# Row sums of the masked attention split between TensorE and GpSimd in the second stack

## The reference

```python
s = einsum(q, k) * scale + rel_bias            # keys by queries
p = exp(s - rowmax)                            # masked keys are 0
o = (p @ v) / sum(p over keys)                 # the row sum is the subject here
```

## Time and profile before

| | |
|---|---|
| three runs, median (lowest to highest) | 2995.5 us (2989.74 to 2997.5) |
| span of the profiled execution | 2989.5 us |
| the run nearest to it | 2989.74 us, 0.24 above the span |
| PE busy | 2868.7 us, 96% |
| DVE, ACT, POOL busy | 1429.5, 1061.5, 245.2 us |
| mean granted clock of PE | 0.973 |
| loops of the stage, first layer and second | from about 1682 to 1825, and from about 2429 to 2572 |

### The profile page before, as it was taken

The page is one execution under the profiler, slowest core; times in us unless marked ns, Lnnn a source line. Parts: engine busy times, 40 slices in busy tenths (PEclk is TensorE's granted clock), DMA queues, the critical chain, the costliest instruction groups (busy, mean ns, idle before and its releaser), DMA issues. The chain is left out here.

```text
span 2989.5 us, 46483 instructions
## 1 busy us (share of the span) xinstructions
PE 2868.7 (96%) x18586; PEld 2453.5 (82%) x18586; DVE 1429.5 (48%) x2279; ACT 1061.5 (36%) x1478; POOL 245.2 (8%) x222
## 2 busy tenths in 40 slices
PE   8999999999999999999999889999999988999998
PEld 7986899999897789999877546788887754678886
DVE  3743477742673267782333654433433355443342
ACT  3244433322334443332333333422323333343232
POOL 1001300001100220001100022000010002200001
PEclk9998999999998999999999889999999988999999
DMA  3200322222220132223232001222222200122222
GB/s 123 99 29 16 133 85 86 92 88 86 76 85 15 43 124 95 84 75 107 88 132 96 29 1 55 86 91 94 98 104 95 96 29 1 57 85 98 92 92 111
DMA packets 44784, 237.04 MB, mean 79 GB/s; under 512 B 4894, under 2 KB 14750, under 8 KB 21872
## 3 DMA queue, kind: packets, MB, share of 16 engines
q1 hardware_dynamic: 34976, 222.09, 21.1%
q10 hardware_dynamic: 9680, 13.17, 1.3%
HBM read 233.09 MB, written 11.59 MB: 82 GB/s over the span
## 5 line engine op out<-in xcount | busy, mean ns | idle before, releaser
L161 PE MATMUL psum<-u_up_a_hi,w_a_hi 128*128 128x264 f32 x1408 | 376.3, 287 | 6.1 <-DVE u_up_a_lo L1900 5.0
L162 PE MATMUL psum<-u_up_a_lo,w_a_hi 128*128 128x264 f32 x1408 | 373.1, 285 | 0.0
L152 DVE TENSOR_TENSOR w_mlp_b_lo<-ring,w_mlp_b_hi 128x1024 fp32r<-128x1024 f32 x128 | 156.9, 1226 | 329.9 <-ACT w_mlp_b_hi L145 329.9
L152 DVE TENSOR_TENSOR w_a_lo<-ring,w_a_hi 128x1024 fp32r<-128x1024 f32 (+1 forms) x154 | 187.6, 1219 | 208.8 <-ACT w_a_hi L145 206.3
L164 PE MATMUL psum<-u_up_a_hi,w_a_lo 128*128 128x264 f32 x1408 | 286.2, 284 | 0.0
L161 PEld LDWEIGHTS psum<-u_up_a_hi,w_a_hi 128*128 128x128 f32 x1408 | 265.1, 188 | 14.2 <-DVE u_up_a_lo L1900 9.7
L145 ACT ACTIVATE w_a_hi<-ring 128x1024 fp32r<-128x1024 f32 (+1 forms) x154 | 161.4, 1049 | 293.4 <-PE psum L164 292.1
L162 PEld LDWEIGHTS psum<-u_up_a_lo,w_a_hi 128*128 128x128 f32 x1408 | 264.7, 188 | 0.1
L145 ACT ACTIVATE w_mlp_b_hi<-ring 128x1024 fp32r<-128x1024 f32 x128 | 135.6, 1060 | 300.4 <-PE psum L164 299.7
L164 PEld LDWEIGHTS psum<-u_up_a_hi,w_a_lo 128*128 128x128 f32 x1408 | 219.4, 189 | 0.0
L161 PE MATMUL psum<-u_up_b_hi,w_mlp_b_hi 128*128 128x512 f32 x512 | 199.6, 390 | 1.0 <-DVE u_up_b_lo L502 1.0
(11 more groups left out here) (459 smaller groups left out, 6505.3 us busy)
## 6 DMA issues: line engine op xcount, KB each, us to landing
ring<-in_wup SPq DMA_DIRECT2D x44, 1024.0 KB, 4.9
ring<-in_wup_b SPq DMA_DIRECT2D x32, 1024.0 KB, 4.8
ring<-in_wdown_b SPq DMA_DIRECT2D x32, 1024.0 KB, 4.8
ring<-in_win SPq DMA_DIRECT2D x22, 1024.0 KB, 4.9
ring<-in_wdown SPq DMA_DIRECT2D x32, 704.0 KB, 4.1
ring<-in_win_b SPq DMA_DIRECT2D x12, 1024.0 KB, 4.8
near_copies<-near_rows ACTq DMA_DIRECT2D x2, 4608.0 KB
ring<-in_wout SPq DMA_DIRECT2D x8, 1024.0 KB, 4.9
```

What stands on the lines that cost most here:

```text
L152: nc.vector.tensor_tensor(W["lo"][:, buf, 0:n], W["tiles"][:, slot, at:at + n], W["hi"][:, buf, 0:n].bitcast(F32), ALU.subtract).then_inc( ...
L161: nc.tensor.matmul(out[c], a_hi, b_hi, start=start, stop=False)
L162: nc.tensor.matmul(out[c], a_hi, b_lo, start=False, stop=False)
```

## The change

A new buffer `acc` holds 256 columns for each of the two heads, which stand for queries 256 to 511. POOL copies step 0's probabilities into its second half and step 1's first 128 columns into its first half. It adds step 1's other 128 columns, and then adds step 2's columns 128 to 383 (`last_sum`). PE no longer reads `prob` for the row sums in steps 0 and 1. In step 2 it reads only the 128 columns that `acc` doesn't cover, in step 3 all 512, and then `acc` (256). That is 896 columns a head and unit.

PE waits in mix(n,3) for POOL's last sum. ACT waits, before it overwrites a buffer of `prob`, until POOL has read it. On POOL `first_sums(n+1)` stands ahead of the multiplication for unit n, and `last_sum(n+1)` right behind that multiplication.

```diff
             def mix(n, step):
+                if step == K - 1:
+                    pe.wait_ge(summed.sem, summed.at(layer, SUMS + 4 * n + 4))
                 pass_waits(pe, S)
-                for bank, at in ((6, (u["v"], u["v"] + 2 * DH)), (7, (u["v"] + DH, u["v"] + DH))):
+                ones = v[:, j, u["v"] + DH:u["v"] + 2 * DH]
+                for h in range(2):
+                    at = u["v"] + 2 * DH * h
+                    mm = nc.tensor.matmul(ps[DH * h:DH * (h + 1), 6, c0:TB], v[:, j, at:at + DH], prob[:, g % 2, h, 0:TB - c0],
+                                          start=(step == 0), stop=(step == K - 1), skip_group_check=True)
+                if step >= 2:
+                    end = TB if step == K - 1 else 2 * P
                     for h in range(2):
-                        mm = nc.tensor.matmul(ps[DH * h:DH * (h + 1), bank, c0:TB], v[:, j, at[h]:at[h] + DH],
-                                              prob[:, g % 2, h, 0:TB - c0],
-                                              start=(step == 0), stop=(step == K - 1), skip_group_check=True)
+                        mm = nc.tensor.matmul(ps[DH * h:DH * (h + 1), 7, c0:end], ones, prob[:, g % 2, h, 0:end - c0],
+                                              start=(step == 2), stop=False, skip_group_check=True)
+                if step == K - 1:
+                    for h in range(2):
+                        mm = nc.tensor.matmul(ps[DH * h:DH * (h + 1), 7, 2 * P:TB], ones, acc[:, h, :],
+                                              start=False, stop=True, skip_group_check=True)
...
             def exponent(n, step):
+                if step == 0 and n:
+                    act.wait_ge(summed.sem, summed.at(layer, SUMS + 4 * n))
+                if step == 2:
+                    act.wait_ge(summed.sem, summed.at(layer, SUMS + 4 * n + 1))
+                if step == 3:
+                    act.wait_ge(summed.sem, summed.at(layer, SUMS + 4 * n + 3))
...
+            def first_sums(n):
+                g = K * n
+                pool.wait_ge(probs.sem, probs.at(layer, g + 1))
+                if n:
+                    pool.wait_ge(mixed.sem, mixed.at(layer, g))
+                nc.gpsimd.tensor_copy(acc[:, :, P:2 * P], prob[:, g % 2, :, 0:P]).then_inc(summed.sem, 1)
+                pool.wait_ge(probs.sem, probs.at(layer, g + 2))
+                nc.gpsimd.tensor_copy(acc[:, :, 0:P], prob[:, (g + 1) % 2, :, 0:P]).then_inc(summed.sem, 1)
+                pool.wait_ge(summed.sem, summed.at(layer, SUMS + g + 1))
+                nc.gpsimd.tensor_tensor(acc[:, :, P:2 * P], acc[:, :, P:2 * P], prob[:, (g + 1) % 2, :, P:2 * P],
+                                        ALU.add).then_inc(summed.sem, 1)
+
+            def last_sum(n):
+                g = K * n
+                pool.wait_ge(probs.sem, probs.at(layer, g + 3))
+                pool.wait_ge(summed.sem, summed.at(layer, SUMS + g + 3))
+                nc.gpsimd.tensor_tensor(acc[:, :, :], acc[:, :, :], prob[:, g % 2, :, P:3 * P], ALU.add).then_inc(summed.sem, 1)
+
+            first_sums(0)
+            last_sum(0)
             for n, u in enumerate(UNITS_B[:-1]):
                 out = part_y[:, :] if u.get("onto") else y[:, u["y"], :]
+                first_sums(n + 1)
                 pool.wait_ge(copied.sem, copied.at(layer, n + 1))
                 pool.wait_ge(inverted.sem, inverted.at(layer, n + 1))
                 then(nc.gpsimd.tensor_tensor(out, out, sums[:, :], ALU.mult))
                 at += 1
+                last_sum(n + 1)
                 if "gate" in u:
...
```

More of the change, by code:

```diff
@@ L2659, in attend_stage_b @@
     side_pe, side_act, side_dve, cleared = S["side_pe"], S["side_act"], S["side_dve"], S["pool_side"]
+    acc, summed, SUMS = M["acc"], S["pool_side"], 6 + 2
     gate_pe, gate_out = S["gate_pe"], S["gate_out"]
@@ L3278, in second_stack @@
             side_pe=signal("side_pe", 8), side_act=signal("side_act", 9), side_dve=signal("side_dve", 21),
-            gate_pe=signal("gate_pe", 6), gate_out=signal("gate_out", 6), pool_side=signal("pool_side", 6 + 2))
+            gate_pe=signal("gate_pe", 6), gate_out=signal("gate_out", 6), pool_side=signal("pool_side", 6 + 2 + 4 * len(UNITS_B)))
         U = len(UNITS_B)
@@ L3317, in mixer @@
                     own = Scope(nc, attention)
-                    for name, shape in (("prob", [P, 2, 2, TB]), ("cn", [P, TB]), ("pc", [P, TB])):
+                    for name, shape in (("prob", [P, 2, 2, TB]), ("cn", [P, TB]), ("pc", [P, TB]), ("acc", [P, 2, TB // 2])):
                         M[name] = own.sb("at_" + name, shape)
```

## The result

The change made the kernel slower: 3028.6 us in the median of 6 runs (3016.1 to 3039.3), against 2996.5 for the kernel before (6 runs, 2989.7 to 2998.6). The ratio on record is 1.0096, 95% interval 1.0075 to 1.0118; the quotient of these two medians, 1.0107, lies inside it. The forecast was 2995, its range 2984 to 3010.

What follows compares the result with a forecast made beforehand. DVE was taken to set the pace from mix(n,0) to mix(n,1), PE's columns from there to mix(n,3). Loop terms summed to -0.2 us a layer, -0.4 for two, from median 2995.5 to 2995; range 2984 to 3010.

Steps and rivals of the forecast that it cites:

- The prediction's own sign of being wrong: Clock falls in the two stages not eight, or POOL's copies and additions taking much more than 0.5, 0.73, 1.28 us.
- Rival 1: Loop 6: PE idles about 3 us ahead of mix(6,3), one more clock fall a layer; 3004.5 us, chance 0.24.
- Rival 2: Loop 5: the thin stretch gets fuller, one clock fall less in each layer; 2985.5 us, chance 0.17.
- Rival 4: PE's columns bound everywhere and POOL hides all; 2983 us, with L3018 down to 2974; chance 0.07.
- Rival 3: DVE's cast is held by POOL's instruction; 3.8 us more, 2999 us, chance 0.17.
- PE's columns at full clock: Steps 1 and 2 each save 0.43 us, step 3 costs 0.43; step 0's 0.21 is worth nothing.
- L3018: DVE's join falls from 0.79 to 0.16 us, 0.63 earlier up to mix(n,1), in loops 1 to 6 and 8.
- The cast: DVE's cast with one SBUF input is taken as not held by POOL; if held, loop 4 is 0.6 us slower.
- POOL's own times: Copies of 256 columns 0.5 us (bounds 0.31 and 0.73), additions 0.73 and 1.28; 3.0 us a unit.
- Loop 3: POOL's gate and addition of unit 2 delay DVE's two-input chain with `select`, and loop 4's bias behind it; +1.0 us.
- The square: `norm_square` waits for POOL's addition onto `y`, now behind the last sum; loop 6 +2.2 us, loop 8 +0.4.
- The end: POOL does gate, addition and low part behind unit 9's last sum, with nothing covering this; +1.8 us.

Runs made afterwards that it cites:

- e5: The kernel before without PE's row sums of steps 0 and 1 (384 of 1280 columns a unit), nothing in their place; ratio 1.0012.
- e14: e5 with constant matmuls of the same length in the places of the columns left out; ratio 1.0015.
- e2: The kernel before with only PE's columns of the change, `acc` holding ones, no POOL work or wait for it; 3020.1 us, ratio 1.0096.
- e13: e9 with PE's columns as in e2; 3004.7 us, ratio 1.0034.
- e9: The kernel before with POOL's multiplication waiting until DVE's join L3018 is over; 2981.2 us, ratio 0.9951.
- e1: The changed kernel's POOL sums and all its waits, but PE's columns as in the kernel before; 3015.9 us, ratio 1.0066.
- e10: e7 with POOL's multiplication also waiting until DVE's splits of the next unit are done, where no square waits for it; ratio 1.0129.
- e6: The kernel before with 256 columns of zeros added to step 3, nothing taken away; ratio 1.0027.
- e7: The changed kernel with POOL's addition onto `y` ahead of the next unit's last sum for units 5 and 7; 3020.6 us, ratio 1.0075.
- e12: e9 with six (loop 7) and four (loop 8) constant matmuls ahead of score(n+1,1), where PE waits for DVE's maxima; 2968.9 us, ratio 0.9902.
- e15: e2 with constant matmuls of the same length in the places of the missing columns in steps 0 to 2; 3035.9 us, ratio 1.0131.
- e3: The changed kernel with three constant matmuls of 128 columns ahead of transposed(n,2); ratio 1.0172.
- e16: The kernel before with only step 2's 256 columns of row sums moved into step 3; 3007.5 us, ratio 1.0031.

## Why the prediction was wrong

**The step that failed** is the sum's silence on the clock: "There are four falls in the loops of a layer", and the sum went by the waits and columns with the falls as they were. In the first layer four became six and in the second four became five, and they grew from 58 to 126 us in all. The prediction's own sign of being wrong came: the falls in the two stages were eleven and not eight. A fall of 10.2 us cost 4.7, 0.46 per us at half clock; 75 us more of it make some 34 us, by the 0.40 of the 88 executions 30, against 27.6 measured in the stages. So the clock is large enough to carry the loss. That taking columns off PE brings the falls about is shown by taking away (e5) and filling again (e14), and by moving (e2, e13 against e9). POOL's waits lose time too (e1, 1.0066), and how the loss of the whole divides between the two halves is open, since they overlap.

**The rivals.** Rival 1 had the right effect, more falls, with the wrong cause, place and size. It put one fall in loop 6, after an idle time of PE of 3 us ahead of mix(6,3), which the wait for POOL was to bring. That idle time was 0.52 us. The falls begin in loop 4, where no idle time of PE ahead of the fall is above 0.90 us, and e2 has them with no wait on POOL at all. Its rule from the Trainium skill (TensorE: Matmul & The Clock Gate, Why this matters for your kernels) warned in the right direction, but speaks of idle gaps; here it was fewer columns in a stream that was already thin. Rival 2 (a fall less in loop 5) did not come in this kernel. Its reasoning was sound for the join alone: e9, with the 0.63 us and all the columns, has no fall in loop 5. Rival 4 (columns are worth 12.8 us) is refuted by e2 and e5. Rival 3 holds: the cast is held. The Trainium skill's GPSIMD Engine Reference (Specifications) names such contention for a 2-port mode; no run shows whether the cast runs in one. The rival's price of 3.8 us was not measured by itself, since e10, which freed the cast, moved other waits.

**PE's columns at full clock.** Forecast -0.43 in loop 2, measured 0.0. The pieces were right (mix of step 0 0.44, step 3 +0.43 by e6, and steps 0 and 1 together -0.44 by e5, which is step 1's part). The error was to count step 2's 0.43 as a gain, though the turning of the maxima right behind it waits for DVE's splits.

**L3018.** Forecast 0.79 to 0.16 and 0.63 a loop; measured 0.164 in the mean, and 0.62 to 0.63 in loop 2 (e1, e9 and after alike). Right, and the best part of the change.

**The cast.** Forecast "not held", by L3011. It was held: 0.70 us in loop 3, 0.78 in loop 4, with L3058 at 1.19 behind it. Nearest was the wrong row: L3011 reads PSUM, the cast SBUF. As rival 3 said, L3058 then waited for a second POOL instruction; it was the gate's (L3245), not the last sum.

**POOL's own times.** Copies 0.40 (forecast 0.5, bounds 0.31 and 0.73), additions 0.73 and 1.27 as forecast. Right.

**Loop 3.** Forecast +1.0, measured +0.25. The first operation of `select` took 1.28 us, held by POOL as described. That the join's gain and slack behind it took up the rest is likely, but no run separates them.

**The square.** Forecast +2.2 in loop 6, of which 1.8 for the wait, and +0.4 in loop 8. ACT stood 3.06 us (forecast about 3): right. For loop 6 as a whole +2.2 was too low, since it grew by 3.4 and 4.1 us in the two layers with a fall of 10.2 us in it, and e7 moved the wait and the fall together. The size of the wait alone is thus not shown there; in loop 8 e7 gave back 0.5.

**The end.** Forecast +1.8, measured +1.60 (9.46 to 11.06; e1 11.06, e2 9.47). Right: it is POOL's work that ends last.

**What stays open** is when exactly the clock falls. e5, e13 and e2 show that work taken from a thin place brings more half clock, e14 and e12 that work put there can take it away. But e9's stretch of 1.45 in 2.50 us had no fall where e13's of 1.52 had one, e15's filler did little, and e3 took one fall and got another. Single executions of one kernel differ as well: those of the kernel before had mean clocks from 0.965 to 0.976. Whether a given edit adds or removes a fall could not be worked out beforehand from any of these profiles.

## What to carry to other kernels

When PE waits for another engine in part of a loop, columns taken off it there can be worth nothing at full clock, and can cost much: 384 columns less per unit brought some 42 us more at half clock over all executions (e5), and the moving of 640 columns some 75 (e2). Before costing such a change at its columns, mark each matmul group by what the next one waits for, and keep a clock fall as a term of the sum wherever the stream is already thin. Compare the clock over all executions and not by one profile: e6's and e16's profiles alone would have blamed columns that do little or nothing to the clock. Look at what a change does on the side: here the order of POOL's work behind one small DVE operation was worth 0.5% alone (e9), and with filler in two waits 1.0% (e12), while the intended part lost 1.0%.

## What the runs showed of the hardware that was not expected

- A DVE cast of 8 columns from SBUF with one input is held by a running POOL instruction (0.17 us free, up to 1.24 us held), and the operation behind it by the next one (0.17 to 1.19). POOL shows nothing of it: its additions took 1.27 us as before. In the rows shown POOL had begun first.
- PE's clock fell to half with no idle time above 0.90 us in the two stretches of 2.5 us ahead, in which PE was busy 1.73 and 1.60 us.
- Six constant matmuls in a wait of PE (1.60 us) shortened loop 7 by 2.4 us, four of them loop 8 by 5.4 (e12). Five of them a unit, put where PE did not wait, cost 0.8 to 1.0 us a loop (e15). In the places of columns that had been taken out, they gave back the clock in e5 (half clock +42 us without, +5 with, in e14), but in e2 only in part, if at all (+75 without, +50 with, in e15).
